# Feed-forward network of a two-layer encoder: column halves that take turns, sums kept in PSUM over a group's end, and a new VectorE and ScalarE order

## The reference

```
f = jnp.square(jax.nn.relu(rms_norm(x, g_ffn_pre) @ w_up)) @ w_down
return x + rms_norm(f, g_ffn_post)
```

## Time and profile before

| | |
|---|---|
| median of 3 runs | 1932.73 us (1932.69 to 1933.38) |
| profiled execution, own time | 1928.0 us |
| its span, first to last instruction | 1925.8 us |
| busy: TensorE (PE), VectorE (DVE), ScalarE (ACT) | 1883.6, 1512.7, 1112.5 us |
| granted TensorE clock, mean | 0.998 of full |

### The profile page before, as it was taken

One profiled execution on the slowest core, in us unless ns is written; L12 is line 12 of the kernel. 1 busy time (PEld: TensorE's weight loads), 2 busy tenths in 40 slices (PEclk: granted clock), 3 DMA queues, 4 the chain that ended last, 5 costly groups with the idle time before them and its releaser, 6 DMA issues.

```text
span 1925.8 us, 28908 instructions
## 1 busy us (share of the span) xinstructions
PE 1883.6 (98%) x9950; PEld 1670.0 (87%) x9950; DVE 1512.7 (79%) x1909; ACT 1112.5 (58%) x1485; POOL 117.7 (6%) x166
## 2 busy tenths in 40 slices
PE   9999999999999999999999999999999999999998
PEld 7988888888987888898888888888789879878987
DVE  6885767897789679787878757778977896797877
ACT  6455656755655564565564556566556556545653
POOL 3920020000000000000000000200000000000000
PEclk9999999999999999999999999999999999999999
DMA  8665357667656656766676544575666666567664
GB/s 288 205 225 168 127 169 275 195 187 234 202 176 210 212 182 194 231 205 207 229 241 215 189 161 148 182 260 172 201 227 193 190 205 215 171 205 232 217 220 153
DMA packets 170065, 390.84 MB, mean 203 GB/s; under 512 B 12160, under 2 KB 14320, under 8 KB 168432
## 3 DMA queue, kind: packets, MB, share of 16 engines
q1 hardware_dynamic: 167904, 377.58, 60.5%
q10 hardware_dynamic: 2064, 12.08, 1.6%
HBM read 382.53 MB, written 7.08 MB: 202 GB/s over the span
## 4 chain that ended last, share of the span: by engine, by line
PE 76%; DVE 13%; issue 4%; DMA 4%; ACT 2%; DVEq 0%; POOL 0%; ACTq 0%; POOLq 0%; SPq 0%
PE acc_pair L568 24%; PE acc_pair L573 12%; PE acc_pair L534 8%; PE acc_pair L535 8%; PE acc_pair L536 8%; DVE w_lo L1439 6%; PE acc_pair L867 3%; PE acc_pair L868 3%; PE acc_pair L869 3%; DMA raw<-in_w_down 3%; DVE kept_sums L2028 1%; DVE t_sum L1996 1%; ACT w_hi L991 1%; DVE t_lo L2007 1%; PE o_bank L786 1%
## 5 line engine op out<-in xcount | busy, mean ns | idle before, releaser
L991 ACT CAST w_hi<-raw 128x1024 fp32r<-128x1024 f32 x687 | 703.9, 1048 | 485.3 <-DVE raw L1992 176.6
L1439 DVE TENSOR_TENSOR w_lo<-raw,w_hi 128x1024 fp32r<-128x1024 f32 x687 | 827.2, 1232 | 157.0 <-ACT w_hi L991 149.5
L568 PE MATMUL acc_pair<-h_both,w_hi 128*128 128x512 f32 x2176 | 560.8, 380 | 3.0 <-DVE acc L1931 1.9
L568 PEld LDWEIGHTS acc_pair<-h_both,w_hi 128*128 128x128 f32 x2176 | 370.9, 190 | 34.9 <-issue 5.3
L573 PEld LDWEIGHTS acc_pair<-h_both,w_lo 128*128 128x128 f32 x2176 | 327.4, 190 | 29.1
L573 PE MATMUL acc_pair<-h_both,w_lo 128*128 128x256 f32 x2176 | 330.4, 274 | 0.0
L867 PE MATMUL acc_pair<-w_hi,f_hi 128*128 128x512 f32 x504 | 191.9, 381 | 15.6 <-DVE acc L1931 10.4
L868 PE MATMUL acc_pair<-w_lo,f_hi 128*128 128x512 f32 x504 | 191.3, 380 | 0.0
L869 PE MATMUL acc_pair<-w_hi,f_lo 128*128 128x512 f32 x504 | 191.1, 379 | 0.0
L534 PE MATMUL acc_pair<-w_hi,h_both 128*128 128x512 f32 x444 | 170.4, 384 | 1.8 <-DVE w_lo L1439 1.2
L535 PE MATMUL acc_pair<-w_lo,h_both 128*128 128x512 f32 x444 | 168.3, 379 | 0.0
(11 more groups left out here) (252 smaller groups left out, 2359.4 us busy)
## 6 DMA issues: line engine op xcount, KB each, us to landing
raw<-in_w_up SPq DMA_DIRECT2D x256, 512.0 KB, 4.5
raw<-in_w_down SPq DMA_DIRECT2D x240, 512.0 KB, 4.8
raw<-in_w_in SPq DMA_DIRECT2D x128, 512.0 KB, 4.9
raw<-in_w_out SPq DMA_DIRECT2D x64, 512.0 KB, 5.3
raw_side<-in_w_down SPq DMA_DIRECT2D x16, 512.0 KB, 7.9
x_kept<-x ACTq DMA_DIRECT2D x4, 1024.0 KB, 7.0
x<-x_kept ACTq DMA_DIRECT2D x4, 1024.0 KB, 6.2
x<-in_x SPq DMA_DIRECT2D x8, 256.0 KB, 8.2
```

What stands on the lines that cost most here:

```text
L568: pe.matmul(acc_pair[b][:, m, :], w_hi[:, slot, col:col + P], x_both.rearrange("p s (a n) -> p s n a", a=2), start=(slot, k) == (0, 0), st ...
L991: act.copy(w_hi[:, half * PAIRS + p, :], raw[:, p, :]).then_inc(hi_made, 1)
L1439: dve.tensor_tensor(w_lo[:, slot, :], src[:, p, :], w_hi[:, slot, :].bitcast(F32), ALU.subtract).then_inc(lo_made, 1)
```

## The change

The number `q` now says which half comes first (0) or second (1) in a group, and `pair_at` says which columns that is: columns 1 then 0 in group 0, 0 then 1 in group 1, 1 then 0 in group 2, and 0 first in group 3, whose narrow units do the rest. The second half of a group and the first of the next have the same columns, so their shared sums go on in the same PSUM banks, and `shared_sums` runs once in each group, after its first half: four times in a layer, the first two of them copies. In the joint between the halves, VectorE's `weight_sums` of place 1 moves behind `wide_sums`. In the last up unit VectorE does `s_rest(3)` before the first `turned_sum`, `weight_sums` of place 1 right after it, the splits of slots 6 and 7 after the second `turned_sum`, and `sums_lo` last. ScalarE takes `s_rest(3)` up front, casts slots 4 and 5 before it takes result b = 1, and slots 6 and 7 right after. The loops over groups 1 and 2 become straight code on SyncE, TensorE, ScalarE and VectorE.

```diff
+def pair_at(g, q):
+    return (q + g + 1) % 2
...
-def shared_done(l, g, j):
-    return SHARED * (l * WIDE_LAYER + g * 2 + j)
+def shared_done(l, g):
+    return SHARED * (l * FF_GROUPS + g + 1)
...
-                load_wide(l, g, 0, hu + 2 * CHUNKS)
+                load_wide(l, g, pair_at(g, 0), hu + 2 * CHUNKS)
...
-                    first, end = n == 0, n == len(SEVEN_AT) - 1
+                    first = n == 0
+                    begin, end = first and (q == 1 or g == 0), n == len(SEVEN_AT) - 1 and q == 0
...
-                    if first and not (isinstance(g, int) and l + g + j == 0):
-                        pe.wait_ge(shared_free, shared_done(l, g, j))
+                    if first and q == 1:
+                        pe.wait_ge(shared_free, shared_done(l, g))
...
+                def last_unit(g, hu):
+                    u = CHUNKS - 1
+                    seven_hi(g, 0, 0, hu + 2, 0)
+                    s_rest(g, 3)
+                    take_half(g, u, 0)
+                    turned_hi(g, u, 0)
+                    act.wait_ge(t_third, seven_no(l, g, 0, 1) + 1)
+                    split_hi(hu + 3, 1, (0, 1))
+                    take_half(g, u, 1)
+                    split_hi(hu + 3, 1, (2, 3))
+                    turned_hi(g, u, 1)
+                    if g == 0:
+                        act.wait_ge(sq_done, l * SQ_LAYER + SQ_H2 + 8)
+                    sums_hi(g, 0, 1)
...
                         shared_sums(g)
                         split_lo(nxt, 0, (2, 3))
-                        weight_sums(g, 1, 1, nxt + 1)
-                        wide_sums(g, j, first)
-                        split_lo(nxt + 1, 1, (0, 1))
-                        sums_lo(g, 1, 1)
-                        split_lo(nxt + 1, 1, (2, 3))
+                        wide_sums(g, q, first)
+                        seven_lo(g, 1, 1, nxt + 1, 1)
...
                     else:
-                        split_lo(nxt, 0, (0, 1))
-                        shared_sums(g, j, first)
-                        split_lo(nxt, 0, (2, 3))
-                        wide_sums(g, j, first)
+                        split_lo(nxt, 0)
+                        wide_sums(g, q, first)
                         split_lo(nxt + 1, 1)
...
+                    def last_unit():
+                        u = CHUNKS - 1
+                        nxt = hu + u * 2 + 2
+                        seven_lo(g, 0, 0, nxt, 0)
+                        s_rest(g, 3)
+                        if first:
+                            mean_x(l, 1, u - 2)
+                        turned_sum(g, u, 0)
+                        weight_sums(g, 0, 1, nxt + 1)
+                        f_stands(g, u, 0)
+                        turned_lo(g, u, 0)
+                        split_lo(nxt + 1, 1, (0, 1))
+                        turned_sum(g, u, 1)
+                        split_lo(nxt + 1, 1, (2, 3))
+                        f_stands(g, u, 1)
+                        turned_lo(g, u, 1)
+                        sums_lo(g, 0, 1)
...
-                group(0, True, False)
-                with dve.Fori(1, FF_GROUPS - 1) as g:
-                    group(g, False, False)
-                group(FF_GROUPS - 1, False, True)
+                for g in range(FF_GROUPS):
+                    group(g, g == 0, g == FF_GROUPS - 1)
```

More of the change, by code:

```diff
@@ L501, in _ @@
                     load_half(w_out, l, 0, c * CH, hu + HU_B2 + c)
-                with sp.Fori(0, FF_GROUPS - 1) as g:
+                for g in range(FF_GROUPS - 1):
                     load_group(l, g)
@@ L884, in seven @@
                     th, tl = t_hi[n % 2], t_lo[n % 2]
-                    if j == 0:
+                    if q == 0:
                         pe.wait_ge(flo_made, l * 32 + g * 8 + k1 // 2 + 1)
                         pe.wait_ge(s_lo_made, (l * FF_GROUPS + g) * len(SEVEN_AT) + n + 1)
-                    if first and not (isinstance(g, int) and l + g + j == 0):
-                        pe.wait_ge(shared_free, shared_done(l, g, j))
+                    if first and q == 1:
+                        pe.wait_ge(shared_free, shared_done(l, g))
                     pe.wait_ge(lo_made, (hu + i // PAIRS) * PAIRS + 2 + RAW)
                     three(ssa_bank[:, :], sh[:, 2, :], sl[:, 2, :], w_hi[:, s0, right],
-                          w_lo[:, s0, right], first, end)
+                          w_lo[:, s0, right], begin, end)
                     three(t_bank[0][:, :], f_hi[:, k0, early], f_lo[:, k0, early], w_hi[:, s0, left],
-                          w_lo[:, s0, left], first, end).then_inc(w_used, 1)
+                          w_lo[:, s0, left], begin, end).then_inc(w_used, 1)
                     def shared_products():
@@ L1424, in group @@
                     act.wait_ge(sq_done, (l + 1) * SQ_LAYER)
-                group(0, True, False)
-                with act.Fori(1, FF_GROUPS - 1) as g:
-                    group(g, False, False)
-                group(FF_GROUPS - 1, False, True)
+                for g in range(FF_GROUPS):
+                    group(g, g == 0, g == FF_GROUPS - 1)
         @block.vector
@@ L1982, in weight_sums @@
                     out = t_sum[n % 2]
-                    again = not (isinstance(g, int) and l + g + j == 0 and n < 2)
+                    again = not (l + g + q == 0 and n < 2)
                     if again:
@@ L2061, in combine, with wide_pair @@
                         dve.wait_ge(q_step, base + 8)
-                def wide_pair(g, j, first, last=False):
-                    hu = hu0 + HU_F + g * HU_GROUP + 2 * CHUNKS + PAIR_HALVES * j
-                    seven_lo(g, j, 2, hu + 2, 0)
-                    seven_lo(g, j, 3, hu + 3, 1)
+                def wide_pair(g, q, first, last=False):
+                    hu = hu0 + HU_F + g * HU_GROUP + 2 * CHUNKS + PAIR_HALVES * q
+                    seven_lo(g, q, 2, hu + 2, 0)
+                    seven_lo(g, q, 3, hu + 3, 1)
                     nxt = hu + PAIR_HALVES
-                    if j == 0 and not last:
+                    if q == 0 and not last:
                         weight_sums(g, 1, 0, nxt)
@@ L2139, in group @@
                         f_chunk_lo(1)
-                        for u in range(1, CHUNKS):
+                        for u in range(1, CHUNKS - 1):
                             turned_unit(u)
                     else:
-                        for u in range(CHUNKS):
+                        for u in range(CHUNKS - 1):
                             turned_unit(u)
```

148 lines of the change are left out of this document (62 added, 86 removed).

## The result

The changed kernel takes 1889.3 us (median of 4 runs, 1889.1 to 1889.8) against 1933.1 us before (4 runs, 1932.7 to 1933.9). The ratio is 0.977, with a 95% interval of 0.976 to 0.979.

A forecast was written before the change was run, and what follows sets the result against it. TensorE, busy 1883.6 of 1925.8 us, was taken as the bound; removing its five kinds of wait on VectorE, together 37.8 us, gives 1932.7 - 37.8 = 1894.9, forecast as 1895 us, range 1891 to 1908.

The forecast's parts named there:

- How the numbers follow: Closing step: profiled time 1890.2 us, median kept 4.7 us above it, so 1895 us; faster 0.93, within 0.2% 0.03, slower 0.04.
- rival 4: Waits merely move, VectorE being the real bound of the down stage; time stays within 0.2%; chance 0.04.
- Part 1: Last up unit reordered: A gone, next weight sums 4.3 us earlier, net VectorE lead at the joint 2.5 to 3.3 us.
- A: TensorE's wait after the up stage for the second `turned_sum`, once in each of 8 groups; 8.1 us to go.
- Part 2: Joint between wide halves: B gone (margin 1.5 us), C gone (margin 1.0 us) by lead and `weight_sums` moved behind `wide_sums`.
- C: TensorE's wait for the first of `wide_sums`, 12 matmuls after B at the 6 joints; 17.2 us to go.
- D: TensorE's wait for `wide_sums` at 6 up-stage starts after a second half; 4.6 us to go.
- B: TensorE's wait for the shared evictions at the 6 joints between two wide halves; 5.3 us to go.
- Part 3: Group's end: 24 evictions fewer save VectorE 14.3 us and remove D, 4.6 us, with a margin of only 0.1 us.
- E: TensorE's wait for `wide_sums` at the 2 starts of the narrow units; 2.6 us to go.
- Part 5: Straight code replacing the group loops: taken as 0, since TensorE shows no wait on its own sequencer at loop ends.
- Rivals 2, 3 and 5: Head start lost, 1904.3, chance 0.17; new wait at place 1, 1903 to 1909, 0.11; straight code starves TensorE, slower, 0.03.

The follow-up runs named there:

- The delays at the joint: Changed kernel with one split repeated on VectorE at each of the six joints: 1917.9 us with four repeats, 1933.8 us with six.

## Why the prediction was wrong

The direction, the mechanism and the sum over the profile held: all five kinds of wait went, and they measure 37.4 us against 37.8. That the whole span came as near (38.5) is partly luck, since 1.7 us of it is one clock fall. What failed is the last part, "How the numbers follow", where it says that the median stays 4.7 us above the profiled execution's own time, "and I keep this distance". In the changed kernel the distance is 0 (1889.4 and 1889.3). It was no constant: the execution profiled before was one with a single clock fall. On the average run of before, the lower clock costs about 5 us, up to 1.7 at a time, and it goes with the waits that the change removes. A term was missing from the sum, put at nothing: what TensorE's waits cost beyond idle time and restart. The delays at the joint show it from the other side, where waits of 4.6 to 5.2 us brought 13.3 us of lower clock with them. The chances for "within 0.2%" and "slower" are also swapped there against rivals 4 and 5 (0.04 and 0.03).

**Part 1** held: A gone, head start 4.5 us measured against the up stage's end (13.1 to 8.5 us; 4.3 worked out). It was undersized in what hangs on it: alone it gives 33 us, not 25, and taken away it costs 30.

**Part 2** held in place, and its margin was too small: 2.5 us measured, where the worked-out lead of 2.5 to 3.3 us gives 1.0 to 1.8. The lead at the joint is 3.9 us (`wide_sums` starts 5.8 us after the half's end before and 0.7 ahead of it now, and 2.6 of that is the order): VectorE did not lose on the way, as the prediction allowed for. One sentence is wrong: that "even with no head start at all" the 2.62 us alone take C away. They do, and most of the time comes back at D and B: 4 us in place of 15.7. In the changed kernel the joint's order is worth 2.5 us. My rival 4, waits that merely move, was nearly right for this part alone; I had weighed it only for the whole.

**Part 3** held: D is gone, worth 4.2 us where the waits went and 4.4 by the kernel without sharing, against 4.6. The margin was as small as it says: `wide_sums` starts at 615.76 at the end of group 1, and 1.64 us on is 617.40, where TensorE starts at 617.50. The 4.6 us are the price of D in straight code and in the kernel before. The new orders with the loops kept leave D at 7.4 us of idle time, and whether sharing removes that too was not tried.

**Part 4** held, E gone, with the head start as its cause (E is back in the kernel with the old last up unit).

**Part 5**, 0 for straight code, is right for the kernel before (0.9994) and wrong beside the new orders, where it is worth 4.1 us. The total did not miss by this, as D had been counted as gone whole. The rule of the Trainium skill ("Runtime: NRT & Kernel Launch", Instruction fetch mechanics) that a taken branch out of the fetched window stalls the engine speaks for a gain by straight code, and there is one; its size in the prediction, a fraction of a microsecond per layer, was worked out from no row. Part of the gain seems to lie in SyncE's issue of loads, and how the rest arises on the other engines was not tried; no trace here shows a fetch.

**Rivals 2, 3 and 5** did not come: no head start lost, no wait at place 1 in any run, no starved TensorE.

Stepwise, by medians over several chips: 1932 to 1934 before; 1898 with both orders; 1893.5 with straight code; 1889.3 with sharing and turns. The steps depend on their order: straight code first is worth nothing.

## What to carry to other kernels

When a wait of the bounding engine goes, ask what it had been giving the engine behind it: VectorE used C to catch up, and without a head start its lateness came back at the next bank wait. Create the head start first, in a stretch where the late engine idles, and then take out what no head start can reach, the work chained behind a last product. Also look at the spread and the granted clock of several executions before carrying a profiled span over to a median.

## What the runs showed of the hardware that was not expected

- Of 24 waits of 2.6 us on TensorE, in four profiles, 12 had 3.4 us at the lower clock at their end, 1.5 to 1.8 us lost each time; waits of 4.6 to 5.2 us had it at all six joints, 13.3 us in all. The longest wait without it was 2.9 us, the shortest with it 1.9.
- A wait costs TensorE its printed idle time and 0.27 us, and over 28 waits this sum (37.8 us) met the matmuls' lateness (37.4) within 0.4 us.
- SyncE's w_down loads in a loop with register addresses leave 0.14 us later than written out, and keep SyncE busy for some 0.22 us more each. In the kernel before this shows in no time (0.9994); beside the new orders it goes with up to 1.8 us.
